# A decoder layer's convolution by parity, its norm's sums in float32r, first tokens in channel halves, MLP entry re-ordered

## The chip, the cores and the metric

The kernel runs on one core of a Trainium2 chip. The metric is the device time of one execution in microseconds (us). Three runs of the kernel before stand behind its median.

## The reference, cut to what matters

One hybrid decoder layer over 2048 tokens of 1024 channels, all in float32. Two token mixers share one input projection: an mLSTM (4 heads of 128, chunks of 128 tokens) and a causal depthwise convolution of width 31 on 512 channels with a norm over groups of 128 channels. Their outputs go through one output projection; a squared-ReLU MLP of hidden size 4096 follows.

```
h_in = rms_norm(x, pre_mix_norm_w); proj = h_in @ w_in
u = conv_val * sigmoid(conv_gate)
u = causal_depthwise_conv(u, conv_w, conv_b)          # width 31
mu = mean over 128 channels; var = mean((u - mu)^2)
y_conv = silu((u - mu) * rsqrt(var + EPS) * conv_norm_w + conv_norm_b)
x = x + rms_norm(concat(y_mlstm, y_conv) @ w_out, post_mix_norm_w)
a = relu(rms_norm(x, pre_mlp_norm_w) @ w_ff1)
x = x + rms_norm((a * a) @ w_ff2, post_mlp_norm_w)
```

## The kernel before, in words

**Arithmetic.** Every large product is made of three float32r products: each operand is rounded to a high part (ScalarE, a copy to float32r) and a low part (VectorE, the operand less its high part), and high x high, high x low and low x high are summed in PSUM. A rounding is thus a step on ScalarE and a following one on VectorE, and a transfer must have landed before.

**Phase A** (to about 590 us) makes the input projection in 96 slots, a list that is written out (SLOTS). Most slots are one PSUM bank of 128 x 512, 24 products of TensorE each. Kinds are qk, gate, val, v, o and ow. TensorE, ScalarE and VectorE each run a loop over the slots in which a function is called at a fixed slot number. ScalarE evacuates each slot but the val ones; VectorE multiplies val by the gate (glu, L811) into the ring u_buf, which has three buffers of 1024 tokens and 30 of the past. A unit is one group of 128 channels by 1024 tokens; there are eight.

**The convolution** of a unit is 31 taps: two on ScalarE (first_tap L624, second_tap L634), 29 on VectorE as operations of 1024 elements that alternate between two sums (tap L829), and one addition (L838). tap_plan (L179) hands taps out to slots: a slot gives VectorE 100 units, a tap costs 23, a weight split or a norm step 22, a q/k convolution 76. CONV_END is the slot in which a unit ends. The norm's steps stand at fixed distances from it (L162): mean sum 1, centring 2, square 3, variance sum 4, root 5, multiplication 6, silu and store to DRAM 7. For the last unit (LAST_UNIT_AT, L163) they are 0, 0, 0, 1, 1, 1, 1. The plan gives CONV_END 22, 29, 41, 49, 60, 68, 79, 87. The sums over 128 channels are float32 products with a matrix of ones (group_sum L500).

**End of phase A.** Slot 91 is CHUNK_0_SLOT. After it TensorE makes the scores of chunk 0 (L537), for which it waits for the last root and for scores_here(0) (L1195): q, k and two row loads, and for the first two chunks also chunk_here (L1191), which counts the loads of v, o and yc. SP loads yc (L1250) when both stores of the convolution's output have landed. Slots 88 to 95 are of kind ow; slot 91 writes the bank of slot 90 and waits for its evacuation.

**Start.** SP issues: x of tokens 0 to 255 (load_first, all channels), the parameters par_a, weight tiles 0 and 1, x of tokens 256 to 511, tiles 2 and 3, then the rest. ScalarE and VectorE wait for par_a, square x in pairs of channel tiles, and split the weight tiles 0 and 1. TensorE fills the wait with warm-up products of ones (WARM = 30), sums the squares, and makes 8 more (WARM_MORE).

**Phase B** (to about 850 us) handles 16 chunks of 128 tokens: mLSTM, output projection in two halves (project), norms, transposes of h2. **Phase C** is the MLP as two stages of seven products of half-sized quadrants (P1 to P7, as by Strassen). The MLP entry is where they overlap: SP loads the token quadrants of the first stage (prefetch["tokens"]), P5 in step 16 of its loop, P2, P3, P6, P7 and P4 in step 17; ScalarE rounds P2 and P3 at the end of step 16 (L1594), VectorE P2 and P3 at the start of step 17 (L1724). TensorE makes P1, the transposes of chunk 14, P2, P3, P6, P7, P4, the last transposes, P5.

**Second stage.** 56 steps, each of 48 products on one part of the hidden values (load_hid L2054, a ring of three). SP issues part 1, the last seven stores of hidden values, then at step n part n + 2 and some weight pieces called grains, which GpSimd adds.

Of the kernel before, what the change touches and what calls it, by code (L numbers as in the profile page):

```python
# [11 lines left out]
P = 128  # L12
S = 2048
# [66 lines left out]
DVE_TAPS = CW - 1  # L80
# [90 lines left out]
WARM, WARM_MORE = 30, 8  # L171
# [3 lines left out]
def convs_at(s):  # L175
    return [q for q in Q_AT if Q_AT[q] == s]


def tap_plan():  # L179
# [5 lines left out]
    for s in range(N_SLOTS):  # L185
        ready = DVE_TAPS * sum(glu_end(u) <= s for u in range(N_UNITS))
# [3 lines left out]
        ends = [min(i for i in range(s) if out[i] >= DVE_TAPS * (u + 1)) for u in range(n // DVE_TAPS)]  # L190
        for u in range(2, N_UNITS):
            if u - 2 >= len(ends) or s < ends[u - 2] + 9:
                ready = min(ready, DVE_TAPS * u)
        more = max(0, min(ready - n, room // TAP_COST))
        for u in range(U_RING, N_UNITS):
            if s + 1 >= glu_slot(u):
                more = max(more, DVE_TAPS * (u - U_RING + 1) - n)
        n += more
        room = min(room - TAP_COST * more, TAP_COST)
# [5 lines left out]

FIRST_TAP = [max(min(s for s in range(N_SLOTS) if TAPS[s] > DVE_TAPS * u) - 1, glu_end(u)) for u in range(N_UNITS)]
CONV_END = [min(s for s in range(N_SLOTS) if TAPS[s] >= DVE_TAPS * (u + 1)) for u in range(N_UNITS)]

SECOND_TAP = [max(FIRST_TAP[u], CONV_END[u - 1] if u else 0) for u in range(N_UNITS)]
# [5 lines left out]
def units_at(s, step):  # L215
    return [u for u in range(N_UNITS) if CONV_END[u] + (step if u < N_UNITS - 1 else LAST_UNIT_AT[step]) == s]
# [30 lines left out]
def phase_a(nc, sem, psum, dram, big, keep, tail):  # L247
# [3 lines left out]
    with ExitStack() as ctx:  # L251
# [9 lines left out]
        u_buf = sb("u_buf", [P, U_RING, CW - 1 + HALF])  # L261
        c_buf = sb("c_buf", [P, 2, HALF])
        th = sb("th", [P, 2, TB])
        sb("pad_a", [P, PAD_A])
# [28 lines left out]
        c_odd = sb("c_odd", [P, HALF])  # L293
        ones, eps = keep["ones"], keep["eps"]
        ln_ps = psum[:, 6:8, :].rearrange("p a b -> p (a b)")

# [38 lines left out]
        def sync(sp):  # L335
# [7 lines left out]
            def load_first(part):  # L343

                at = slice(part * PART, (part + 1) * PART)
                sp.dma_start(big["raw"][:, :, at], dram["xt"][:, :, at]).then_inc(sem["x_in"][part], 16)

            def load_x(tb):
                for half in range(2):
                    kt = slice(half * KT // 2, (half + 1) * KT // 2)  # L350
                    sp.dma_start(x_at(tb, kt), dram["xt"][:, kt, tb * TB:(tb + 1) * TB]).then_inc(sem["x_in"][2 * tb + half], 16)
# [21 lines left out]
        def tensor(pe):  # L373
# [5 lines left out]
            def sum_part(part, kt):  # L379
# [4 lines left out]
                elif kt < KT // 2:  # L384
                    pe.wait_ge(sem["x_sq"], kt // 2 + 1)
                else:
                    pe.wait_ge(sem["x_sq_dve"], (kt - KT // 2) // 2 + 1)
# [124 lines left out]
            for s in range(6, N_SLOTS):  # L512
                slot(s)
                for u in units_at(s, AT_MEAN):
                    pe.wait_ge(sem["tap"], DVE_TAPS * (u + 1))
# [4 lines left out]
                    for b in range(2):  # L520
                        group_sum(c_buf[:, u % 2], b)
# [26 lines left out]
        def scalar(act):  # L548
            def square_pair(q, part):
                act.wait_ge(sem["x_in"][part], 16)  # L550
# [73 lines left out]
            def first_tap(u):  # L624
# [1968 lines left out]
```

## Time and profile before

| | us |
|---|---|
| median of 3 runs (2085.43 to 2087.7) | 2086.36 |
| the profiled execution, its own time | 2085.33 |
| its span, first to last instruction | 2083.5 |
| TensorE busy | 2067.1 |
| VectorE busy | 1446.1 |
| ScalarE busy | 912.1 |
| GpSimd busy | 417.2 |
| mean granted TensorE clock | 0.998 |

The span lacks 1.8 us of the execution's own time, which lies around it. Products on TensorE are pipelined: a row's duration is longer than the distance to the next one, and that distance (the pitch) is what a product costs.

### The profile page before, as it was taken

The numbers are of one execution on the slowest core, as the hardware profiler recorded it, in microseconds if no ns is written. First come the engines' busy times: TensorE is split into PE (matmuls) and PEld (weight loads), VectorE is DVE, ScalarE is ACT, GpSimd is POOL, SyncE is SP. The second block draws the span as 40 slices with busy tenths as digits, with TensorE's granted clock in tenths as the row PEclk, the third lists the DMA queues.
The fourth block names the chain that finished last, engine by engine and source line by source line (L and its number), as shares of the span: only waits on it lengthen the run. The fifth ranks groups of instructions, "written<-read, shape, count | busy, mean of one in ns | idle before, by whom it ended". The sixth has DMA issues, their size and how long they took to land. (4 is left out here: it accounts for less than half of the span.)

```text
span 2083.5 us, 26901 instructions
## 1 busy us (share of the span) xinstructions
PE 2067.1 (99%) x10031; PEld 1734.2 (83%) x10031; DVE 1446.1 (69%) x1993; ACT 912.1 (44%) x1557; POOL 417.2 (20%) x252
## 2 busy tenths in 40 slices
PE   9999999999999999999999999999999999999998
PEld 8897878878788888788888888888788888888887
DVE  6897999989567777886666976666563536624285
ACT  6632434343454445754555654455331313313163
POOL 0000000000002323352332333232353134400012
PEclk9999999999999999999999999999999999999999
DMA  5121212113656875765446755545756455543376
GB/s 204 32 87 47 70 41 81 51 32 105 199 177 195 266 235 171 266 192 167 137 142 191 236 171 156 167 150 189 245 210 259 154 193 202 174 169 126 138 257 218
DMA packets 254144, 338.55 MB, mean 162 GB/s; under 512 B 11584, under 2 KB 195648, under 8 KB 240192
## 3 DMA queue, kind: packets, MB, share of 16 engines
q1 hardware_dynamic: 221376, 315.80, 45.6%
q10 hardware_dynamic: 32384, 20.98, 3.2%
q8 instruction: 81, 1.33, 0.3%
q14 instruction: 47, 0.39, 0.1%
q0 software_dynamic: 256, 0.07, 0.0%
HBM read 225.58 MB, written 111.21 MB: 162 GB/s over the span
## 5 line engine op out<-in xcount | busy, mean ns | idle before, releaser
L1978 PE MATMUL psum<-x_hi,w_hi_P 128*128 128x512 f32 x896 | 349.8, 390 | 3.8 <-DVE x_lo L1922 2.4
L2198 PE MATMUL psum<-w_hi,hid_hi 128*128 128x512 f32 x896 | 348.8, 389 | 1.9 <-DVE hid_lo L2074 1.9
L1978 PE MATMUL psum<-x_lo,w_hi_P 128*128 128x512 f32 x896 | 349.1, 390 | 0.0
L1978 PE MATMUL psum<-x_hi,w_lo_P 128*128 128x512 f32 x896 | 349.1, 390 | 0.0
L2198 PE MATMUL psum<-w_hi,hid_lo 128*128 128x512 f32 x896 | 348.6, 389 | 0.0
L2198 PE MATMUL psum<-w_lo,hid_hi 128*128 128x512 f32 x896 | 348.6, 389 | 0.0
L2074 DVE TENSOR_TENSOR hid_lo<-hid_raw,hid_hi 128x1024 fp32r<-128x1024 f32 x112 | 174.4, 1593 | 211.4 <-ACT hid_hi L2069 211.4
L1891 POOL TENSOR_TENSOR w_raw<-w_raw 128x512 f32<-128x512 f32 x128 | 184.9, 1467 | 395.3 <-DVE w_lo_P L1904 345.8
L2069 ACT ACTIVATE hid_hi<-hid_raw 128x1024 fp32r<-128x1024 f32 x112 | 112.9, 1051 | 343.4 <-DMA hid_raw<-scratch_hid 343.3
L1904 DVE TENSOR_TENSOR w_lo_P<-w_raw,w_hi_P 128x512 fp32r<-128x512 f32 x224 | 184.1, 834 | 98.1 <-ACT w_hi_P L1900 95.5
L1900 ACT ACTIVATE w_hi_P<-w_raw 128x512 fp32r<-128x512 f32 x224 | 136.0, 626 | 236.8 <-PE psum L1978 227.2
L1978 PEld LDWEIGHTS psum<-x_hi,w_hi_P 128*128 128x128 f32 x896 | 168.4, 188 | 40.4 <-issue 5.9
L2198 PEld LDWEIGHTS psum<-w_hi,hid_hi 128*128 128x128 f32 x896 | 168.2, 188 | 37.5 <-issue 2.7
L1978 PEld LDWEIGHTS psum<-x_hi,w_lo_P 128*128 128x128 f32 x896 | 168.5, 188 | 35.5
L1978 PEld LDWEIGHTS psum<-x_lo,w_hi_P 128*128 128x128 f32 x896 | 168.6, 188 | 34.7
L2198 PEld LDWEIGHTS psum<-w_hi,hid_lo 128*128 128x128 f32 x896 | 168.2, 188 | 35.0
L2198 PEld LDWEIGHTS psum<-w_lo,hid_hi 128*128 128x128 f32 x896 | 168.2, 188 | 34.9
L2030 POOL TENSOR_TENSOR w_raw<-w_raw,w_grain 128x1024 f32<-128x1024 f32 x48 | 137.9, 2888 | 224.5 <-DMA w_grain<-in_w 224.5
L841 DVE SCALAR_TENSOR_TENSOR c_buf<-u_buf,par_a,c_buf 128x1024 f32<-128x1024 f32 x120 | 153.2, 1276 | 0.0
L841 DVE SCALAR_TENSOR_TENSOR c_odd<-u_buf,par_a,c_odd 128x1024 f32<-128x1024 f32 x112 | 142.9, 1276 | 5.2 <-ACT c_odd L638 5.2
L404 PE MATMUL psum<-big_hi,w_hi 128*128 128x512 f32 (+1 forms) x288 | 109.0, 378 | 0.8 <-DVE big_lo L795 0.7
L2323 DVE TENSOR_TENSOR c<-c,psum 128x512 f32<-128x512 f32 x96 | 65.4, 681 | 61.9 <-PE psum L1978 61.9
(284 smaller groups left out, 3820.0 us busy)
## 6 DMA issues: line engine op xcount, KB each, us to landing
scratch_hid<-stage SPq DMA_DIRECT2D x224, 256.0 KB, 3.7
hid_raw<-scratch_hid SPq DMA_DIRECT2D x56, 1024.0 KB, 4.9
w_raw<-in_w SPq DMA_DIRECT2D x52, 1024.0 KB, 5.0
w_grain<-in_w SPq DMA_DIRECT2D x48, 512.0 KB, 5.3
x_raw<-scratch_h2s SPq DMA_DIRECT2D x14, 1024.0 KB, 8.4
w_raw<-in_w_in SPq DMA_DIRECT2D x22, 512.0 KB, 3.6
scratch_h2s<-h2s SPq DMA_DIRECT2D x8, 1280.0 KB, 10.1
scratch_qk<-qout ACTq DMA_DIRECT2D x16, 512.0 KB, 3.3
```

What stands on the lines that cost most here:

```text
L404: mm = nc.tensor.matmul(out, a, b, start=kt == 0 and i == 0, stop=kt == KT - 1 and i == 2)
L841: nc.vector.scalar_tensor_tensor(out=out, in0=u_buf[:, u % U_RING, k:k + HALF], scalar=par[:, CONV_W + g * CW + k:CONV_W + g * CW + k + 1] ...
L1891: nc.gpsimd.tensor_tensor(raw_1(op), raw_1(a), raw_1(b), ALU.subtract).then_inc(sem["w1_t"], 1)
L1900: nc.scalar.activation(w1_hi[op][:], raw_1(op), ACT.Copy).then_inc(sem["w1_hi"], 1)
L1904: nc.vector.tensor_tensor(w1_lo[op][:], raw_1(op), w1_hi[op][:].bitcast(F32), ALU.subtract).then_inc(sem["w1_lo"], 1)
L1978: mm = nc.tensor.matmul(psum[:, bank_1(op, g), :], l, r, start=kt == 0 and i == 0, stop=kt == 3 and i == 2)
L2030: nc.gpsimd.tensor_tensor(part, part, grain[:, n % 2], alu).then_inc(sem["w2_t"], 1)
L2069: nc.scalar.activation(hid_hi[n % HID_RING][:, half_fps(h)], hid_raw[n % HID_RING][:, half_fps(h)], ACT.Copy).then_inc(sem["hid_hi"], 1)
L2074: nc.vector.tensor_tensor(hid_lo[n % HID_RING][:, half_fps(h)], hid_raw[n % HID_RING][:, half_fps(h)], hid_hi[n % HID_RING][:, half_fps(h) ...
L2198: mm = nc.tensor.matmul(psum[:, bank, :], l, r, start=f == 0 and k == 0, stop=f == NFP - 1 and k == 2)
L2323: nc.vector.tensor_tensor(out[:], a[:], ps1(op, g), ALU.add).then_inc(sem["gather"], 1)
```

## The change

It does the following.

- The convolution works on even and odd tokens apart. u_buf holds the two halves of a unit one after the other (glu writes them with a stride). With a = even taps on even tokens, b = odd taps on odd tokens, and m = (sums of tap pairs) on (sums of token pairs), even outputs are a + b and odd outputs m - a' - b. A unit is 48 steps on VectorE with 512 or 513 elements (527 for the first) in place of 30 with 1024: S (token pairs), 15 A, 14 B, 15 M, E, T, O. Three first taps are on ScalarE. The planner charges 12.6 a step.
- The norm's sums are float32r: u is rounded to a high part (ScalarE) and a low part (VectorE), summed in two products per bank each; the same for the squares. The high part lies in the ring of u, so glu waits for the sums of three units ago, not for its taps.
- The steps stand at other distances; the planner charges four norm steps in place of one. Silu writes tokens back in order, with a stride, into another buffer.
- The first 256 tokens come as two transfers of four channel tiles each from a copy in DRAM of their own; tile 0 of the weights is loaded and split ahead of them; ScalarE squares pairs 0 and 2, VectorE 1 and 3; squares don't wait for par_a. WARM is 18.
- MLP entry: P5's tokens are loaded last; P2 is rounded earlier, on ScalarE after the squares of the first half of chunk 15, on VectorE between the two halves of post_scale. Second stage: hidden part 2 is issued before the last stores; the grains for the second product start one step later.

```
-DVE_TAPS = CW - 1
+EVEN, ODD = (CW + 1) // 2, CW // 2
+UH = HALF // 2
+UX = UH + EVEN
...
-AT_MEAN, AT_CENTER, AT_SQUARE, AT_VAR, AT_RSTD, AT_NORM, AT_SILU = 1, 2, 3, 4, 5, 6, 7
-LAST_UNIT_AT = {AT_MEAN: 0, AT_CENTER: 0, AT_SQUARE: 0, AT_VAR: 1, AT_RSTD: 1, AT_NORM: 1, AT_SILU: 1}
+UNIT_AT = {AT_HIGH: 0, AT_SUM_HIGH: 1, AT_LOW: 1, AT_SUM_LOW: 2, AT_CENTER: 2, AT_SQUARE: 3, AT_SQUARE_LOW: 3,
+           AT_VAR: 5, AT_RSTD: 6, AT_NORM: 7, AT_SILU: 8}
+LAST_UNIT_AT = {AT_HIGH: 0, AT_SUM_HIGH: 1, AT_LOW: 1, AT_SUM_LOW: 2, AT_CENTER: 2, AT_SQUARE: 2, AT_SQUARE_LOW: 2,
+                AT_VAR: 3, AT_RSTD: 3, AT_NORM: 3, AT_SILU: 3}
-TAP_COST = 23
+STEP_COST = 12.6
-WARM, WARM_MORE = 30, 8
+WARM, WARM_MORE = 18, 8
...
+    out = [("S", 0)]
+    for j in range(1, EVEN):
+        out += [("A", j)] + ([("B", j)] if j < ODD else []) + ([("M", j - 1)] if j > 1 else [])
+    return out + [("E", 0), ("M", EVEN - 1), ("T", 0), ("O", 0)]
...
-            room -= 22 * sum(out[s - AT_NORM] >= DVE_TAPS * (u + 1) > out[s - AT_NORM - 1] for u in range(N_UNITS))
+            for at in (AT_LOW, AT_CENTER, AT_SQUARE_LOW, AT_NORM):
+                room -= 22 * sum(out[s - UNIT_AT[at]] >= N_STEPS * (u + 1) > out[s - UNIT_AT[at] - 1] for u in range(N_UNITS))
...
-            if u - 2 >= len(ends) or s < ends[u - 2] + 9:
+            if u - 2 >= len(ends) or s < ends[u - 2] + 10:
...
+                for half, landed in enumerate((sem["x_in"][0], sem["x_head"])) if part == 0 else ():
+                    kt = slice(half * KT // 2, (half + 1) * KT // 2)
+                    sp.dma_start(big["raw"][:, kt, at], dram["x_first"][0, :, kt]).then_inc(landed, 16)
...
+            load_w(0)
             load_first(0)
             sp.dma_start(par[:], dram["params_a"]).then_inc(sem["par_a"], 16)
-            load_w(0)
             load_w(1)
...
-            def group_sum(src, b):
-                nc.tensor.matmul(psum[:, 6 + b, :], ones[:], src[:, b * TB:(b + 1) * TB],
-                                 start=True, stop=True).then_inc(sem["ln_sum"], 1)
+            def group_sum(src, b, start, stop):
+                return nc.tensor.matmul(psum[:, 6 + b, :], ones_r[:], src[:, b * TB:(b + 1) * TB], start=start, stop=stop)
...
                 for u in units_at(s, AT_VAR):
-                    pe.wait_ge(sem["c_sq"], u + 1)
+                    pe.wait_ge(sem["ln_act"], 3 * u + 3)
+                    pe.wait_ge(sem["ln_dve"], 3 * u + 3)
                     for b in range(2):
-                        group_sum(rstd, b)
+                        group_sum(high_part(u), b, True, False)
+                        group_sum(square_low, b, False, True).then_inc(sem["ln_sum"], 1)
...
                 if tb % 2 == 0 and u >= U_RING:
-                    dve.wait_ge(sem["tap"], DVE_TAPS * (u - U_RING + 1))
+                    dve.wait_ge(sem["ln_sum"], LN_SUMS * (u - U_RING + 1))
...
+                nc.vector.scalar_tensor_tensor(out=a_sum, in0=u_halves(u)[:, 0, j:j + UH + 1],
+                                               scalar=par[:, CONV_W + g * CW + 2 * j:CONV_W + g * CW + 2 * j + 1],
+                                               in1=a_sum, op0=ALU.mult, op1=ALU.add).then_inc(sem["tap"], 1)
...
+                    for name in ("scores", "qs", "z", "incr", "y", "yc_lo"):
+                        sp.wait_ge(sem[name], NCH - 1)
+                    prefetch["tokens"](sp, OPS[6:])
...
                     do["squares"](c - 1, 0)
+                if c == NCH:
+                    prefetch["high_x"](act, "P2")
                 if 2 <= c < NCH + 2:
                     do["pre_mlp"](c - 2)
...
                 if c == NCH + 1:
-                    prefetch["low_x"](dve, "P2")
                     prefetch["low_x"](dve, "P3")
...
                     do["post_scale"](c - 1, 0)
+                    if c == NCH:
+                        prefetch["low_x"](dve, "P2")
                     do["post_scale"](c - 1, 1)
...
         load_hid(sp, 1)
+        load_hid(sp, 2)
         store(sp, NGRP - 1)
...
-            if n + 2 < NSTEP:
+            if 1 <= n and n + 2 < NSTEP:
                 load_hid(sp, n + 2)
...
-                    if (j * 6 // n_grains if op not in WHOLE else 1 + j * 5 // n_grains) == m:
+                    if (1 + j * 5 // n_grains if op in WHOLE else 1 + j * 6 // n_grains if i == 0 else j * 6 // n_grains) == m:
```

## Rows read from the trace of the kernel before

**Rows 1.** The page, its first part: TensorE's busy time and share.

```profile
PE 2067.1 (99%) x10031; PEld 1734.2 (83%) x10031; DVE 1446.1 (69%) x1993; ACT 912.1 (44%) x1557; POOL 417.2 (20%) x252
```

**Rows 2.** Who waited for whom, TensorE: us in total, times, longest.

```profile
PE psum L1978 <- DVE x_lo L1922: 2.4, 2, 2.2
PE psum L2198 <- DVE hid_lo L2074: 1.9, 2, 0.9
PE psum L501 <- DVE c_buf L838: 1.1, 3, 0.8
```

**Rows 3.** Timeline of TensorE, 156 to 163 us: start, us, what.

```profile
157.74 1.88 PE L501 MATMUL psum<-c_buf,ones 128*128 128x512 f32 x4
...
159.68 0.39 PE L404 MATMUL psum<-big_lo,w_hi 128*128 128x512 f32 x1
159.91 0.39 PE L404 MATMUL psum<-big_hi,w_lo 128*128 128x512 f32 x1
```

**Rows 4.** Timeline of VectorE, two taps of unit 0 after each other.

```profile
113.33 1.28 DVE L841 SCALAR_TENSOR_TENSOR c_buf<-u_buf,par_a,c_buf 128x1024 f32<-128x1024 f32 x1
114.53 1.28 DVE L841 SCALAR_TENSOR_TENSOR c_odd<-u_buf,par_a,c_odd 128x1024 f32<-128x1024 f32 x1
```

**Rows 5.** VectorE by line (busy us, mean ns, idle before); then busy time from 95 to 540 us.

```profile
L800 DVE SCALAR_TENSOR_TENSOR x_raw<-x_raw,par_a,rstd_a 128x512 f32<-128x512 f32 x16 | 11.7, 744 | 8.2 <-ACT rstd_a L571 8.2
...
95.00:540.00 445.00, 443.86 (x2400) 377.47 (x2399) 398.01 (x368) 166.80 (x193) 4.15 (x10) 1.00 0.22 69
```

**Rows 6.** Timeline of TensorE, end of slot 87 and slot 91 to the scores.

```profile
537.95 0.39 PE L480 MATMUL psum<-w_hi,big_lo 128*128 128x512 f32 x1
...
559.97 0.47 PE L480 MATMUL psum<-w_hi,h_hi 128*128 128x512 f32 x1 [0.78 <-ACT th L615]
...
565.54 1.06 PE L1389 MATMUL psum<-q_t,k_t 128*128 128x128 f32 x8
```

**Rows 7.** Timelines of ScalarE, SP and VectorE: slot 88's evacuation to the exponents.

```profile
546.58 0.60 ACT L615 ACTIVATE th<-psum 128x512 f32<-128x512 f32 x1 [3.15 <-PE psum L480]
...
552.39 1.25 ACT L713 ACTIVATE c_buf<-c_buf,par_a 128x1024 f32<-128x1024 f32 x1
...
557.91 0.80 SPq L1250 DMA_DIRECT2D yc_c<-scratch_yc  x2
...
560.79 2.25 DVE L1207 SCALAR_TENSOR_TENSOR p_c<-negm_b,cols,mask 128x128 f32<-128x128 f32 x4 [8.46 <-DMA yc_c<-scratch_yc]
```

**Rows 8.** MLP entry: TensorE, VectorE; busy time by engine, PEclk, DMA, GB/s.

```profile
853.92 0.47 PE L1978 MATMUL psum<-x_hi,w_hi_P 128*128 128x512 f32 x1 [2.21 <-DVE x_lo L1922]
...
874.30 0.47 PE L1978 MATMUL psum<-x_hi,w_hi_P 128*128 128x512 f32 x1 [0.66 <-DVE h2s L1699]
...
851.16 0.32 DVE L1670 TENSOR_TENSOR small<-small 128x1 f32<-128x1 f32 x1 [1.75 <-ACT junk L1529]
...
852.11 6.16 DVE L1922 TENSOR_TENSOR x_lo<-x_raw,x_hi 128x1024 fp32r<-128x1024 f32 x4
...
854.00:858.40 4.40, 4.39 (x12) 3.04 (x13) 4.40 (x4) 3.31 (x5) 0.92 (x1) 0.61 1.05 387
```

**Rows 9.** Timelines at the start: TensorE, ScalarE, VectorE.

```profile
9.87 1.99 PE L388 MATMUL psum<-c_buf,ones 128*128 128x256 f32 x8
...
9.19 1.16 ACT L551 ACTIVATE c_buf<-big_raw 128x512 f32<-128x512 f32 x2 [7.16 <-DMA par_a<-in_params_a]
...
10.49 1.06 ACT L581 ACTIVATE w_hi<-w_raw 128x1024 fp32r<-128x1024 f32 x1 [0.15 <-DMA w_raw<-in_w_in]
...
11.82 1.06 ACT L581 ACTIVATE w_hi<-w_raw 128x1024 fp32r<-128x1024 f32 x1 [0.27 <-DMA w_raw<-in_w_in]
...
14.59 0.88 DVE L800 SCALAR_TENSOR_TENSOR big_raw<-big_raw,par_a,rstd_a 128x256 f32<-128x256 f32 x2 [0.45 <-ACT rstd_a L571]
```

**Rows 10.** Second stage: TensorE's third step; SP's issue of hidden part 2.

```profile
1488.51 0.47 PE L2198 MATMUL psum<-w_hi,hid_hi 128*128 128x512 f32 x1 [0.93 <-DVE hid_lo L2074]
...
1479.87 0.72 SPq L2062 DMA_DIRECT2D hid_raw<-scratch_hid  x1
```

More of the change, by code:

```diff
@@ L513, in tensor @@
                 slot(s)
-                for u in units_at(s, AT_MEAN):
-                    pe.wait_ge(sem["tap"], DVE_TAPS * (u + 1))
+                for u in units_at(s, AT_SUM_HIGH):
+                    pe.wait_ge(sem["ln_act"], 3 * u + 1)
                     if u == 0:
@@ L549, in square_pair @@
             def square_pair(q, part):
-                act.wait_ge(sem["x_in"][part], 16)
+                if part == 0 and q >= KT // 4:
+                    act.wait_ge(sem["x_head"], 16)
+                else:
+                    act.wait_ge(sem["x_in"][part], 16)
                 nc.scalar.activation(x_sq_pair(q, part), x_pair(q, part), ACT.Square).then_inc(sem["x_sq"], 1)
@@ L718, in scalar @@
                     act.dma_start(dram["yc"][chunks(half), :, g, :].rearrange("c p t -> p c t"),
-                                  c_buf[:, u % 2].rearrange("p (c t) -> p c t", t=P)).then_inc(sem["c_out"][u % 2], 16)
+                                  c_tokens(u)[:].rearrange("p (c t) -> p c t", t=P)).then_inc(sem["c_out"][u % 2], 16)
+                for u in range(N_UNITS):
+                    if FIRST_TAP[u] == s:
+                        first_taps(u)
+                    if PAIR_TAP[u] == s:
+                        pair_tap(u)
                 for j, half in convs_at(s - 2):
@@ new lines, in odd_tap @@
+            def odd_tap(u, j):
+                g = u // 2
+                if j == 1:
+                    dve.wait_ge(sem["tap0"], 3 * u + 2)
+                else:
+                    dve.wait_ge(sem["tap"], step_done(u, "B", j - 1))
+                nc.vector.scalar_tensor_tensor(out=b_sum, in0=u_halves(u)[:, 1, j:j + UH],
+                                               scalar=par[:, CONV_W + g * CW + 2 * j + 1:CONV_W + g * CW + 2 * j + 2],
+                                               in1=b_sum, op0=ALU.mult, op1=ALU.add).then_inc(sem["tap"], 1)
@@ new lines, in pair_tap, with add_pairs @@
+            def pair_tap(u, j):
+                if j == 1:
+                    dve.wait_ge(sem["tap0"], 3 * u + 3)
+                else:
+                    dve.wait_ge(sem["tap"], step_done(u, "M", j - 1))
+                nc.vector.scalar_tensor_tensor(out=m_sum(u), in0=u_pairs(u)[:, j:j + UH], scalar=pair_weight(u // 2, j),
+                                               in1=m_sum(u), op0=ALU.mult, op1=ALU.add).then_inc(sem["tap"], 1)
+            def add_pairs(u):
+                dve.wait_ge(sem["evac"]["dve"], 2 * (u + 1))
+                if u >= 1:
+                    dve.wait_ge(sem["tap"], step_done(u - 1, "M", EVEN - 1))
+                nc.vector.tensor_tensor(u_pairs(u), u_halves(u)[:, 0, 1:UX], u_halves(u)[:, 1, 0:UX - 1],
+                                        ALU.add).then_inc(sem["tap"], 1)
@@ new lines, in even_tokens, with both_sums, odd_tokens @@
+            def even_tokens(u):
+                dve.wait_ge(sem["tap"], step_done(u, "A", EVEN - 1))
+                nc.vector.tensor_tensor(c_buf[:, u % 2, 0:UH], a_sum[:, 0:UH], b_sum, ALU.add).then_inc(sem["tap"], 1)
+            def both_sums(u):
+                dve.wait_ge(sem["tap"], step_done(u, "E"))
+                nc.vector.tensor_tensor(b_sum, a_sum[:, 1:UH + 1], b_sum, ALU.add).then_inc(sem["tap"], 1)
+            def odd_tokens(u):
+                dve.wait_ge(sem["tap"], step_done(u, "T"))
+                nc.vector.tensor_tensor(m_sum(u), m_sum(u), b_sum, ALU.subtract).then_inc(sem["tap"], 1)
@@ new lines, in add_weights @@
+            def add_weights():
+                taps = par[:, CONV_W:CONV_W + H * CW].rearrange("p (g k) -> p g k", g=H)
+                sums = pairs[:, 0:H * EVEN].rearrange("p (g j) -> p g j", g=H)
+                nc.vector.tensor_tensor(sums[:, :, 0:ODD], taps[:, :, 0:CW - 1:2], taps[:, :, 1:CW - 1:2], ALU.add)
+                nc.vector.tensor_copy(sums[:, :, ODD:EVEN], taps[:, :, CW - 1:CW])
+                link(nc.vector.tensor_scalar(pairs[:, H * EVEN:H * EVEN + H], par[:, CONV_B:CONV_B + H], 2.0, None, ALU.mult))
@@ L863, in vector @@
                 nc.vector.memset(qk_raw(j, 0)[:, 0:QW - 1], 0.0).then_inc(sem["q_head"], 1)
-            for q in range(KT // 4, KT // 2):
-                square_pair(q)
-            split_w(0)
             split_w(1)
@@ L1324, in sync @@
                     load_x(c)
-                if c == NCH:
-                    for name in ("scores", "qs", "z", "incr", "y", "yc_lo"):
-                        sp.wait_ge(sem[name], NCH - 1)
-                    prefetch["tokens"](sp, OPS[6:])
                 if c == NCH // 2:
```

215 lines of the change are left out of this document (141 added, 74 removed).

## The prediction

> **What bounds the kernel now.** I read the page's first part first: TensorE is busy for 99% of the span [rows 1]. So a change pays only where it removes TensorE work or one of its few waits. The waits of TensorE [rows 2] name three places that the change touches: the MLP entry (2.4 us), the start of the second MLP stage (1.9 us) and the sums of the convolution's norm (1.1 us). VectorE has slack: 398.0 us busy of 445 us between 95 and 540 us [rows 5]. A cheaper convolution on VectorE is therefore worth nothing by itself.
>
> **Norm sums, seven units.** A float32 sum is two recorded passes. Four records, that is two sums, start at 157.74; the second L404 product starts at 159.68 and one pitch before that is 159.45, so two sums hold TensorE for 1.71 us, 0.855 us each [rows 3]. The float32r products follow each other at 0.23 us (159.68 to 159.91). A unit now has 4 sums, two for the mean and two for the variance, 3.42 us. It gets 8 float32r products, 8 x 0.23 = 1.84 us. Gain 1.6 us a unit, 11.2 us for units 0 to 6. Of the 1.1 us of waits for c_buf [rows 2], 0.3 us belong to them and go, since the sums now stand one slot later.
>
> **The last unit.** Here the change adds a wait. Walking the planner's loop with 48 steps at 12.6 and the four norm charges, the convolution of unit 7 still ends in slot 87. Before, its variance sum stood after slot 88 and its silu in slot 88. After, high, low, two mean steps and the low square are in between: variance, root and silu stand in slot 90. Chunk 0's scores stay after slot 91, and scores_here makes TensorE wait for chunk_here(0), which counts the load of yc, which starts when the silu has been stored. The chain from the evacuation of slot 88 to the landing is 546.58 to 560.79, 14.2 us, with silu at 552.39 and the load's issue at 557.91 [rows 7]. TensorE had 19 us for it and came 4.7 us late (565.54 [rows 6]). Now it hangs on slot 90, and TensorE needs from there 0.9 us for four sums (these cover the 0.78 us for which it now waits for the evacuation) and 5.6 us for slot 91 (559.97 to 565.54 [rows 6]), 6.5 us: **it waits about 7.7 us**. As a whole: before, end of slot 87 (537.95 + 0.23) to the scores is 27.4 us. After: 3 slots x 5.5 + 4 early products 0.9 + 14.2 = 31.6 us. Loss 4.2 us, this unit's cheaper sums and the vanished 0.8 us wait included. Queued behind on SP are the second half of w_out (needed two slots later, covered) and on POOL and VectorE scale_q and the exponents, which then run beside slot 92.
>
> An idle TensorE also loses its clock: after the gap that ended at 853.92 the granted clock of 854 to 858.4 was 0.61 in the mean, so the lower level (1.2 GHz) lay over some 0.78 x 4.4 = 3.4 us, 1.7 us lost [rows 8]. I add 1.7 us behind the longer gap: +5.9 us in all. The Trainium skill (TensorE: Matmul & The Clock Gate, "What's actually happening") says the same from the other side: throttled is the default and only activity releases it. Without that rule and row the sum would be 1.7 us lower.
>
> **VectorE and the ring of u.** A unit's taps go from 30 operations of 1.28 us, which follow each other at 1.20 us [rows 4], about 36 us, to 48 of half the length. The nearest row is a 512-element one with a column scalar, 744 ns [rows 5]; less the same 0.08 us of overlap 0.66 us, about 31.5 us a unit. The two added 1024-long subtractions (no more than 1.2 us each, the pitch of a tap of that length) leave 2 us of gain a unit, all in slack. ScalarE gets two roundings of 1.06 us [rows 9] a unit and saves half a us, also slack. But glu of slot 45 must now wait for the sums of unit 2, which stand after slot 46, because the high part lies in the ring of u. Behind it queue 20 steps of unit 3 (13 us), the glu of slot 47, a weight split and a norm. Counted through, unit 3 ends some 6 us into slot 50, and TensorE waits for its rounding after slot 50: between 0 and 3 us, I take 1.0.
>
> **Start.** The sums of the first 256 tokens begin at 9.87, when par_a (9.19) has landed, and w tile 0 is there at 10.49, tile 1 at 11.82 [rows 9]. After, tile 0 goes ahead of x, squares wait for x halves only and not for par_a, and both roundings of tile 0 lie ahead of them; but ScalarE's root stands behind the rounding of tile 1. If transfers keep their pace, tile 1 lands at 11.8 as now, the root follows at 12.9 and VectorE can normalise at 14.1 instead of 14.59: 0.5 us. If the smaller first transfer lets the queue start quicker, up to 3.3 us. Against it: 18 warm-up products instead of 30 end near 6.4 us; with the sums at 9.4 the clock would have fallen, which costs up to 1.5 us in place of a gain. I take a gain of 1.5, ends -1.5 and +3.3. The split into halves in DRAM costs nothing: rows in SBUF stay 1 KB.
>
> **MLP entry.** TensorE waits 2.21 us until 853.92 for the low part of P2, then runs partly at the low clock, then waits 0.66 us before 874.30 for VectorE's h2s [rows 8]. P5's load (1 MB; at the 387 GB/s of this stretch [rows 8] 2.7 us) goes behind P4's, so P2 lands 2.7 us earlier than now; its rounding fits into ScalarE's idle time before pre_mlp(14), or delays it by up to 1 us. From 852.11 to 874 us VectorE is busy almost without a break, and the same work remains. What it can give back is its 1.75 us of idle time before 851.16 [rows 8], no more; PE's 2.2 us and the clock are then paid by later small waits. Gain 1.75, ends 0 and 3.9 (all of gap and clock). P5's own roundings come 15 us later and don't notice.
>
> **Second stage.** Hidden part 2 is issued at 1479.87 behind seven stores and lands so late that TensorE starts at 1488.51 after 0.93 us [rows 10]; part 3 the same. Issued ahead of the stores and of the grains, both are early: -1.9 us. The grains move back one step and still end before step 7, when their roundings start.
>
> **Sum.** -11.2 -0.3 +5.9 +1.0 -1.5 -1.75 -1.9 = -9.75 us. The profiled execution took 2085.33 us (span 2083.5, 1.8 us around it), so 2075.6; the median of the runs is 1.0 us above it: **2076.5 us**.
>
> **Rivals.** (1) *No wait at the scores*: if the yc chain is hidden (a load that I count wrongly, a planner end some slots earlier), the seam gives 1.6 + 0.8 + 0.8 us instead of costing 5.9: 2067.5 us. For it: 4.7 us of slack now. Against it: two slots of 5.5 us eat more than that. Chance 0.18. (2) *Small gain*: start loses 1.5, the entry gives nothing, unit 3's wait is 3: -9.75 + 3.0 + 1.75 + 2.0 = -3.0, 2083 us. Chance 0.09. (3) *VectorE becomes the bound, slower*: the half-length taps cost more than the planner's 12.6% of a 5.47 us slot (0.69 us), and every unit's high part is late for its sum. The nearest row gives 0.66 us, so only 4% lie between. 384 steps at 0.80 are 54 us more than mine; against 47 us idle time now, 16 us gained and more synchronising waits, some 20 us would reach TensorE: about 2095 us. It decides from about 0.75 us a step. The Trainium skill (VectorE: DVE Perf Modes, "The TRN2 errata") speaks against short operations, since each pays a fixed latency anew. The rows have that term as 2 x 0.744 - 1.28 = 0.21 us, and 0.66 us includes it; hence only 0.05.
>
> **Numbers.** Forecast case 0.68. The range takes in rivals 1 and 2: 2065 to 2083. About 0.2%, 4.2 us, is what a measurement of this kernel tells from no change. Faster: forecast and rival 1, 0.86 less a tail, 0.85; within: 0.10; slower: 0.05.
>
> **What would show it.** Norm sums in float32r at some 0.23 us pitch, 64 of them; a TensorE gap of 6 to 9 us before L1389's first score ended by yc or what waits for it, and the lower clock level behind it; no gap at 1488 or 1500; the P2 product right behind its transposes, small waits for x_lo of P3 to P7 instead; steps at 0.66 us. Wrong would be: no gap at the scores (then 2067), or waits for the high part in every unit (then slower).

## The result: slower by 0.6%, and the profile after

The changed kernel takes 2098.14 us (median of 4 runs, 2097.42 to 2100.17), the kernel before beside it 2086.56: ratio 1.0058, 95% interval [1.0046, 1.007]. The forecast was 2076.5 us, so the change is slower by 11.6 us where it was to be faster by 10. The profiled execution of after has a span of 2097.0 us against 2083.5.

The page of after, its first part, against [rows 1]: TensorE has 6 us less to do and VectorE 14 us less, and still the span is 13.5 us longer.

```profile
PE 2060.8 (98%) x10007; PEld 1740.2 (83%) x10007; DVE 1432.2 (68%) x2164; ACT 929.0 (44%) x1581; POOL 419.0 (20%) x252
```

The waits of TensorE in after (us in total, times, longest), against [rows 2]: the 1.1 us before the norm's sums have become 18.4 us in three lines, there is a new wait at the scores, and the wait for the hidden part is gone.

```profile
PE psum L558 <- DVE u_high L1038: 8.5, 3, 5.9
PE psum L558 <- ACT u_high L770: 5.5, 3, 3.6
PE psum L1544 <- DMA yc_c<-scratch_yc: 5.3, 1, 5.3
PE psum L558 <- DVE square_low L1046: 4.4, 1, 4.4
PE psum L2135 <- DVE x_lo L2079: 1.8, 1, 1.8
```

The timeline of TensorE gives the large ones their places: unit 4's high sum, unit 6's low sum, unit 7's variance sums, the scores.

```profile
380.42 1.22 PE L558 MATMUL psum<-u_high,ones 128*128 128x512 f32 x2 [3.59 <-ACT u_high L770]
...
506.76 1.22 PE L558 MATMUL psum<-u_high,ones 128*128 128x512 f32 x2 [5.90 <-DVE u_high L1038]
507.78 0.41 PE L546 MATMUL psum<-w_hi,big_hi 128*128 128x256 f32 x1
507.99 0.41 PE L546 MATMUL psum<-w_lo,big_hi 128*128 128x256 f32 x1
...
512.58 0.28 PE L546 MATMUL psum<-w_hi,big_hi 128*128 128x256 f32 x1
512.70 0.28 PE L546 MATMUL psum<-w_lo,big_hi 128*128 128x256 f32 x1
...
566.48 0.50 PE L558 MATMUL psum<-high_last,ones 128*128 128x512 f32 x1 [4.40 <-DVE square_low L1046]
...
579.96 1.40 PE L1544 MATMUL psum<-q_t,k_t 128*128 128x128 f32 x5 [5.28 <-DMA yc_c<-scratch_yc]
```

The four products in the middle show the clock. Behind the 5.9 us gap products of 256 columns follow each other at 0.21 us, from about 512.2 us on at 0.12 us. These are the two levels, 1.2 and 2.4 GHz. The granted clock was 0.5 for 6.8 us from 379.1, 6.8 from 505.3, 3.4 from 566.8 and 6.8 from 577.0. Windows of after say the same (the last three columns are PEclk, DMA share, GB/s):

```profile
505.00:513.00 8.00, 6.24 (x30) 6.05 (x31) 8.00 (x11) 1.15 (x1) 0.14 (x2) 0.57 0.31 98
566.00:570.00 4.00, 3.52 (x9) 2.84 (x10) 0.33 (x1) 2.90 (x3) 0.00 (x0) 0.60 0.18 66
577.00:584.00 7.00, 4.04 (x16) 3.81 (x17) 2.91 (x5) 1.74 (x6) 1.26 (x1) 0.51 0.76 237
```

**Where the 13.5 us of span are**, from start times of the same products in both traces. To the first product: 16.12 to 14.20, -1.9 us. From there to the scores (565.54 and 579.96): +16.3. Scores to the first product of MLP stage 1 (847.57 and 863.87): +1.9, in it the low clock behind the scores' gap. Stage 1: -0.4. Stage 2: -2.5. So all of the loss is made between the first product and the scores. There the waits for sums grew by 17.3 and the scores' by 5.3 us, cheaper sums gave 8 x 1.6 = 12.8 back, one wait of 0.8 went, and 7.3 us are left. The low clock explains 6.4 of them, 0.9 us stay unexplained: of its first 17.1 us TensorE worked through 14.3, and a product took 0.213 instead of 0.118 us, so 0.45 of that time is lost. Of the last 6.8 us, 3.9 lie behind the scores and explain 1.7 of the 1.9 us there.

The rows that answer to [rows 4], [rows 8] and [rows 9]: two kinds of half-length steps on VectorE (by line), then TensorE's first product, and its first P2 product at the MLP entry.

```profile
L920 DVE SCALAR_TENSOR_TENSOR ab_buf<-u_buf,par_a,ab_buf 128x513 f32<-128x513 f32 x120 | 90.0, 750 | 4.0 <-ACT ab_buf L695 4.0
L931 DVE SCALAR_TENSOR_TENSOR ab_buf<-u_buf,par_a,ab_buf 128x512 f32<-128x512 f32 x112 | 83.8, 748 | 0.0
```

```profile
14.20 0.36 PE L461 MATMUL psum<-big_hi,w_hi 128*128 128x256 f32 x1 [0.84 <-DVE big_lo L877]
...
873.36 0.47 PE L2135 MATMUL psum<-x_hi,w_hi_P 128*128 128x512 f32 x1 [1.80 <-DVE x_lo L2079]
```

The steps have the duration that was forecast, the first product comes 1.9 us earlier, and the wait at the entry is still 1.8 us. The wait that was in [rows 10] has no row in after.

### The profile page after: what moved, and what is told of

Read it like the earlier page. It is cut to its first block, busy times and chain, and to the rows that moved or that the text cites. A ratio compares the mean times of both kernels' runs of the same rounds, so it can differ in the third digit from the quotient of the medians.

```text
span 2097.0 us, 27079 instructions
## 1 busy us (share of the span) xinstructions
PE 2060.8 (98%) x10007; PEld 1740.2 (83%) x10007; DVE 1432.2 (68%) x2164; ACT 929.0 (44%) x1581; POOL 419.0 (20%) x252
## 4 chain that ended last, share of the span: by engine, by line
PE 57%; DVE 1%; issue 0%; ACT 0%; DVEq 0%; ACTq 0%
PE psum L2356 29%; PE psum L2135 28%; DVE x_lo L2079 0%; DVE w_lo_P L2061 0%; DVE c L2481 0%; DVE c_x L2481 0%; ACT x_hi L2072 0%; ACT junk L1693 0%; DVE xn L1838 0%; DVE h2s L1855 0%; DVE acc L2562 0%; DVE acc L2540 0%; DVEq L2703 0%; ACT rs_c L2411 0%; ACT junk_c L2438 0%
## 5 line engine op out<-in xcount | busy, mean ns | idle before, releaser
L461 PE MATMUL psum<-big_lo,w_hi 128*128 128x512 f32 (+1 forms) x288 | 105.3, 366 | 0.0
L461 PE MATMUL psum<-big_hi,w_lo 128*128 128x512 f32 (+1 forms) x288 | 105.3, 366 | 0.0
```

Source lines behind the costliest of these rows:

```text
L461: mm = nc.tensor.matmul(out, a, b, start=kt == 0 and i == 0, stop=kt == KT - 1 and i == 2)
```

## Experiments

The table has for each run the time from the first product (L404 of before) to the first score in its profiled execution, the stretch in which all of the loss is made, beside the median. The other stretches, the start aside, differ by 2.5 us at most. With the new start the first product comes between 13.0 and 14.3 us, which differs from execution to execution. The kernel before, run beside each group, had medians from 2085.7 to 2086.6 us (2086.2 is that of all its runs), so medians of different groups compare to about 1 us.

| run | what it is | first product to scores, us | median, us |
|---|---|---|---|
| before | | 549.4 | 2086.2 |
| after | | 565.8 | 2098.1 |
| e1 | start, entry, stage 2 only | 550.4 | 2082.3 |
| e2 | after, float32 sums | 550.9 | 2082.0 |
| e3 | after, float32 sums in unit 7 | 560.2 | 2088.7 |
| e4 | after, own root buffer in unit 7 | 564.8 | 2096.3 |
| e5 | e3 + filled gaps | 556.3 | 2088.7 |
| e6 | e3 + low part earlier in its slot | 552.4 | 2083.3 |
| e7 | e3 + joint mean sum | 555.9 | 2087.0 |
| e8 | e3 + q/k ahead of first taps | 560.6 | 2090.6 |
| e9 | e6 + VectorE's load cut | 537.1 | 2067.9 |
| e10 | e6 + q/k stored from the raw rows | 542.4 | 2073.6 |
| e11 | e7 + the same | 544.8 | 2074.9 |
| e12 | after + the same | 556.1 | 2089.3 |
| e13 | e1 + the same | 548.4 | 2079.0 |

The theory at the start: the sums in float32r are what loses, since each unit's mean now goes ScalarE, TensorE, VectorE, TensorE (each step a handshake with the next) with one slot between, on queues served in order. Rivals: the parity convolution puts VectorE late; the seam, the stretch from unit 7's end to the scores, is late by its DMA; the re-ordered loads cost something.

**e1, all of the change but convolution and norm.** The kernel before with only the edits of start, MLP entry and second stage:

```diff
+ sp.dma_start(big["raw"][:, kt, at], dram["x_first"][0, :, kt]).then_inc(landed, 16)
...
+ if c == NCH:
+     prefetch["high_x"](act, "P2")
...
+ load_hid(sp, 2)
```

> The kernel before with the change's start, MLP entry and second-stage edits only; convolution and norm as before. Theory (the loss is made by the convolution's and norm's part alone): the start gives 1.9 us (first product at 14.2 instead of 16.1), the second stage 1.9, the entry 0 to 1.5, so 2081 to 2083 us, and a clock below full only behind the entry. Rival (some of the loss is made by the moved loads): 2086 us or more.

Measured 2082.29 us, ratio 0.998 [0.9971, 0.9989]. As expected: these parts are worth 4 us, and none of the loss is theirs.

**e2, the parity convolution with float32 sums.**

```diff
- group_sum(high_part(u), b, True, False).then_inc(sem["ln_sum"], 1)
+ exact_sum(c_buf[:, u % 2], b).then_inc(sem["ln_sum"], 2)
...
+ root_last = ab_buf[:, 0:HALF]
```

> The changed kernel with the parity convolution, but the norm's sums taken in float32 straight from the float32 tiles in all 8 units, at the slots of the kernel before (no high and low parts, variance 4 slots after the convolution's end, last unit 0 and 1 slots after it); the last unit's squares and root stand in the buffer of the two partial sums, so that they don't wait for the store of unit 6. Theory (handshakes of the split sums make the waits, the half-length steps are harmless): all of the 18 us of waits for sums and the 5 us at the scores go, and with them the low clock of phase A; what stays is the gain of start and second stage: 2081 to 2084 us. Rival (the parity convolution itself puts VectorE late): waits of several us for the sums of units 3 to 7 remain, 2088 us or more.

Measured 2081.98 us, 0.998 [0.9971, 0.9989], the same as e1. The parity convolution neither helps nor hurts by itself with float32 sums, and the float32r sums with their slots and buffers, cheaper by 12.8 us, cost 16 us net.

**e3, float32 sums for the last unit alone.** The same edit with `exact(u)` true for unit 7 only.

> The changed kernel with float32 sums, at the slots of the kernel before, for the last unit only (its squares and root in their own buffer as in the run above); units 0 to 6 keep the split sums. Theory: the 4.4 us before the variance sums and the 5.3 us before the scores go, with some 3 to 5 us of low clock, against 1.6 us more for the sums: 2086 to 2090 us; the waits of units 2 to 6 (14 us) and their low clock stay. Rival (the seam is late because unit 7's convolution is late, whatever its sums are): 2094 us or more, with a wait of over 4 us at the sums or scores.

Measured 2088.71 us, 1.0012 [1.0003, 1.0021]: of the 16 us the seam makes 9.4. By the profiles it is 7.8: 5.6 up to the scores and 2.2 between the scores and MLP stage 1. From unit 7's first sum to the scores it takes 26.4 us again (546.83 to 573.26), as before (539.09 to 565.54), against 29.95 in after, where the first sum also stands a slot later. e3 is the base for the runs that follow.

**e4, without the wait for unit 6's store.**

```diff
- nc.scalar.activation(rstd[:], c_buf[:, u % 2], ACT.Square).then_inc(sem["ln_act"], 1)
+ nc.scalar.activation(root(u), c_buf[:, u % 2], ACT.Square).then_inc(sem["ln_act"], 1)
...
+ sp.wait_ge(sem["c_out"][0], 16 * (N_UNITS // 2))
```

> The changed kernel with one wait removed: squares, low squares and root of the last unit stand in the buffer of the two partial sums instead of the one from which unit 6 is stored, so ScalarE's squares no longer wait 6.2 us for that store to land; the k load of the tail waits for the store instead. Theory (that store is what makes the variance sums 4.4 us late): variance sums on time, the scores' wait falls to 0 to 5 us, some of the low clock goes: 2088 to 2093 us. Rival (the handshakes are late by themselves, or the yc load is): within 2 us of the changed kernel.

A miss: 2096.29 us, 1.0049 [1.0037, 1.0062], only 1.9 us better. The timeline of after shows the wait that it takes away, and the waits of e4 show why little came of it: the variance sums were on time, but the scores then waited longer for yc.

```profile
562.93 1.06 ACT L776 ACTIVATE rstd_a<-c_buf 128x1024 f32<-128x1024 f32 x1 [6.17 <-DMA scratch_yc<-rstd_a]
565.11 1.23 DVE L1046 TENSOR_TENSOR square_low<-rstd_a,high_last 128x1024 fp32r<-128x1024 f32 x1 [7.25 <-ACT high_last L779]
```

```profile
PE psum L1554 <- DMA yc_c<-scratch_yc: 7.3, 1, 7.3
```

From unit 7's first sum to the scores e4 needs 27.4 us and after 29.95, so the store's wait is worth 2.5 us there. (The table shows 1.0, since this execution of e4 had 3.4 us more of low clock, at unit 3.) The rest of the seam's loss stays without the store's wait, and e3, with the sums and slots of the kernel before, has none of it. That fits the seam's length in slots, as the prediction had it.

**e5, the low clock taken away, the waits left.** In three gaps of e3 products of the tile of ones fill TensorE's time:

```diff
+ if u == 4:
+     fill(s, 14)
...
+ if u in (3, 6):
+     fill(s, 7 if u == 3 else 24)
```

> Base: the run with float32 sums for the last unit only (2088.7 us). In the three largest gaps that TensorE has there before a norm sum (unit 3's low sum 1.9 us, unit 4's high sum 3.7 us, unit 6's low sum 5.9 us) 7, 14 and 24 products of the tile of ones with itself are put ahead of the wait; they write a free bank and change no result. The waits end when they ended before. Theory (the idle gaps also cost the clock behind them: 17 us at 0.5 in that run): the low stretches go and 6 to 9 us with them, 2080 to 2083 us. Rival (the low clock costs next to nothing, what counts is the waits alone): 2087 us or more.

Measured 2088.70 us, 1.0014 [1.0005, 1.0023]: nothing, by the medians. Yet the edit did what it was meant to: the windows below, of e3 first and then of e5, have a granted clock of 0.89 and 0.81 against 1.00 and 0.95.

```profile
370.00:400.00 30.00, 26.19 (x179) 24.75 (x178) 26.50 (x42) 8.21 (x11) 0.00 (x0) 0.89 0.18 50
497.00:515.00 18.00, 12.12 (x79) 11.72 (x78) 12.43 (x14) 5.58 (x7) 0.14 (x2) 0.81 0.28 87
```

```profile
370.00:400.00 30.00, 28.60 (x212) 26.72 (x211) 27.34 (x46) 7.48 (x10) 0.00 (x0) 1.00 0.21 70
497.00:515.00 18.00, 18.00 (x147) 17.91 (x147) 13.36 (x16) 5.24 (x7) 0.14 (x2) 0.95 0.28 88
```

In e3 the clock was low for 17 us of the stretch up to the scores, and TensorE worked through 14.8 of them; in e5 it was low for 3.4. At the pitches above some 5 us of TensorE's time came back. By the profiles, from the first product to the scores e5 is 3.9 us shorter. Part of the rest is the edit's own: the fill ahead of unit 6's low sum runs 0.7 us past the end of the low part. And part is waited away. From unit 4's high sum to unit 6's, e3 has a low stretch that costs 2.6 us and e5 has none, yet both need 114.1 to 114.2 us. In e5 TensorE meets these waits, where e3 has none and one of 1.0 us:

```profile
387.88 0.73 PE L576 MATMUL psum<-u_high,ones 128*128 128x512 f32 x2 [1.28 <-DVE u_high L1083]
...
494.31 0.73 PE L576 MATMUL psum<-u_high,ones 128*128 128x512 f32 x2 [2.12 <-ACT u_high L812]
```

Why the 3.9 us don't show in the medians stays open. In the profiled execution of e5 the first product comes 1.2 us later than in e3's and MLP stage 1 takes 1.8 us more, both outside the edit, and its runs scatter (2086.7 to 2092.5). My theory in its first form, waits plus clock, has no place for a gain that is waited away. **The second theory:** between unit 2 and unit 7 VectorE's queue sets the pace, by its work plus forced waits; what TensorE gains there is waited away at a later sum. The waits of VectorE from 95 to 545 us, in the kernel before and in after, show what there is:

```profile
DVE u_buf L825 <- PE psum L404: 25.8, 11, 7.6
DVE qout L852 <- ACT qout L649: 13.2, 8, 4.3
```

```profile
DVE qout L1000 <- ACT qout L719: 29.4, 8, 7.8
DVE u_buf L910 <- PE psum L461: 8.5, 4, 4.2
DVE u_buf L910 <- issue: 7.9, 3, 5.0
DVE u_buf L903 <- PE psum L558: 7.5, 1, 7.5
DVE square_low L1046 <- ACT u_high L779: 6.2, 3, 3.4
```

VectorE is busy 21 us less than before in this stretch (399.2 and 378.2 us), but before it mostly waited for TensorE to finish a glu slot (25.8 us), which costs nothing. Now it waits for qout, for the ring of u, for the squares. And the timelines of ScalarE and VectorE show the wait for qout from inside, at unit 6:

```profile
493.26 1.06 ACT L770 ACTIVATE u_high<-c_buf 128x1024 fp32r<-128x1024 f32 x1 [5.03 <-DVE c_buf L965]
...
496.25 1.14 ACT L725 ACTIVATE qout<-qout,par_a 128x1024 f32<-128x1024 f32 x1
497.42 0.37 ACTq L728 DMA_DIRECT2D scratch_qk<-qout  x1
500.46 1.15 ACT L719 ACTIVATE qout<-qraw,par_a 128x1024 f32<-128x1024 f32 x1 [3.07 <-DMA scratch_qk<-qout]
```

```profile
501.64 3.92 DVE L1000 SCALAR_TENSOR_TENSOR qout<-qraw,par_a,qout 128x1024 f32<-128x1024 f32 x3 [7.80 <-ACT qout L719]
505.49 1.22 DVE L1038 TENSOR_TENSOR u_high<-c_buf,u_high 128x1024 fp32r<-128x1024 f32 x1
```

ScalarE waits 5.0 us for the convolution's last step, because the rounding of the high part stands first in its slot. Queued behind it are three first taps and the silu of the q/k convolution before. Its store goes out at 497.4, and the next first tap, into the same qout, waits for it to land. VectorE waits 7.8 us for that tap, and only then comes the low part for which TensorE has waited since 500.9. The next runs test links of this chain.

**e6, the low part ahead of the q/k convolution.**

```diff
+ for u in split_at(s, AT_LOW):
+     dve.wait_ge(sem["ln_sum"], LN_SUMS * u + 2)
  for j, half in convs_at(s - 1):
      convolve_qk(j, half)
```

> Base: as above, 2088.7 us. One thing moved: on VectorE the low part of units 0 to 6 stands ahead of the q/k convolution of its slot, not behind it. Theory (unit 6's 5.9 us and unit 3's 1.9 us are a low part queued behind a q/k convolution, which itself waits for ScalarE's first tap and so for the store of qout): both waits go, and the low clock of 506 us and 318 us: 2078 to 2082 us; unit 4's 3.7 us for the high part stay. Rival (VectorE is simply behind, the order doesn't matter): 2087 us or more, the waits stay.

Measured 2083.31 us, 0.9986 [0.9978, 0.9995], 5.4 us less than e3 and 1.3 us above the expected range. The waits at units 3 and 6 went, but TensorE was earlier and met another one, at unit 7's mean sum:

```profile
PE psum L576 <- ACT u_high L800: 5.4, 3, 3.5
PE psum L579 <- issue: 5.1, 1, 5.1
```

**e7, two handshakes fewer.** The low part goes into the buffer of the roots and all four mean sums stand together:

```diff
- nc.vector.tensor_tensor(high_part(u), c_buf[:, u % 2], high_part(u).bitcast(F32),
+ dve.wait_ge(sem["c_out"][(u - 1) % 2], 16 * ((u - 1) // 2 + 1))
+ nc.vector.tensor_tensor(square_low[:], c_buf[:, u % 2], high_part(u).bitcast(F32),
```

> Base: as above, 2088.7 us. The split mean sum with two handshakes fewer: the low part goes into the buffer of the roots instead of over the high part, so that it need not wait for the sums of the high part; it stands ahead of the q/k convolution; all four sums of the mean stand together 2 slots after the convolution's end, so the high part has two slots and the low part one. Nothing else of units 0 to 6 moves. Theory: all waits of units 2 to 6 (14 us) and their low clock (8 us) go, 2066 to 2073 us, below both kernels. Rival (a wait in another form takes their place, for the store of the unit before which the roots' buffer must see landed, or the ring): 2078 us or more.

A miss: 2087.04 us, 1.0003 [0.9994, 1.0012], 17 us above the middle of what I expected. TensorE's waits for sums are no shorter than in e6, in other places (7.9 us in three, 5.2 at unit 7), and VectorE waits 7.8 us for the store of the unit before. More room in slots for the handshake did not help here. The edit also added the wait for the store, so e7 alone does not show which of the two undid the gain.

**e8, the first taps behind q/k on ScalarE**, in the order of the kernel before:

```diff
  for j, half in convs_at(s):
      first_tap_qk(j, half)
+ for u in range(N_UNITS):
+     if FIRST_TAP[u] == s:
+         first_taps(u)
```

> Base: as above, 2088.7 us. One thing moved: on ScalarE the first taps of a unit stand behind the q/k silu, store and first tap of the slot, as in the kernel before, not ahead of them. Theory (VectorE idles 29 us for qout's first tap instead of 13 us because the store that this tap waits for is issued later): VectorE's idle time for qout falls by 10 us or more, unit 4's high part is earlier by some of it, 2083 to 2087 us. Rival (these waits are the store's own time, or the steps wait for the first taps instead): within 1.5 us of 2088.7.

Measured 2090.55 us, 1.0018 [1.0009, 1.0026]: no gain. The 1.8 us above e3 lie within the scatter of its runs (2086.2 to 2091.7). VectorE's idle time for qout fell only from 31.2 to 27.8 us.

**e9, VectorE with less to do.**

```diff
+ b = b_sum[:, 0:64] if j >= 8 else b_sum
...
+ m = m_sum(u)[:, 0:64] if j >= 8 else m_sum(u)
```

> Base: the run with the low part ahead of the q/k convolution (2083.3 us). Left out: of the odd taps and of the pair taps with number 8 and up, in all units, only the first 64 of 512 columns are computed; number, order and waits of the instructions stay. VectorE has some 15 x 0.6 = 8 us less to do in a unit, TensorE and ScalarE the same as in the base. Theory (between units 2 and 7 it is VectorE's in-order work with its forced waits that sets when the high part and unit 7's mean sum can come; what TensorE saved in the sums turned up there as waits, 3.5 us at unit 4 and 5.1 us at unit 7): these waits go, with their low clock, 2069 to 2074 us. Rival (the waits come from the slots in which the steps stand, not from VectorE's load): 2081 us or more.

The kernel leaves out seven eighths of the columns of 15 taps in each unit; VectorE is busy for 325 us between 95 and 545 us, against 380 in e6. Measured 2067.94 us, 0.9915 [0.9901, 0.9929], 15.4 us below e6 and a little below what was expected. From the first product to the scores it takes 13.3 us less than e1: seven units' cheaper sums (11.2 us) and e1's waits for c_buf (2.2 us). What TensorE still waits for at the sums of units 0 to 6 in the whole trace is one row:

```profile
PE psum L576 <- DVE u_high L1071: 0.5, 1, 0.5
```

Nothing was changed but VectorE's load: the handshakes, the slots and ScalarE's queue are those of e6. So in e6 VectorE, its work plus its forced waits, is the bound of this stretch, and 2068 us is about what these sums are worth when it isn't. Its waits by themselves cost nothing once it has time for them: the one for qout is longer here than in e6 (22.7 us), and the one for the ring of u is 7.5 us in both.

```profile
DVE qout L1035 <- ACT qout L749: 34.2, 10, 6.8
```

**e10, the q/k store no longer blocks qout.**

```diff
- nc.scalar.activation(qout[:], qout[:], ACT.Silu,
+ nc.scalar.activation(qk_raw(j, half)[:, QW - 1:QW - 1 + HALF], qout[:], ACT.Silu,
...
- act.wait_ge(sem["q_out"], 16 * (2 * j + half))
+ act.wait_ge(sem["q_silu"], 2 * j + half)
```

> Base: as above, 2083.3 us. The silu of a q/k convolution writes into the raw rows that it came from, and is stored from there; ScalarE's next first tap into qout no longer waits for the store before it, only the next fill of the raw rows does. VectorE idled 23 us in the base for that tap, 13 us in the kernel before. Theory (as above, and this wait is a part of it that can be removed): VectorE's idle time for qout falls to under 15 us, the waits at unit 4's high part and unit 7's mean sum (3.5 and 5.1 us) shrink by half or more, 2074 to 2080 us. Rival (VectorE idles there because TensorE has not finished the slot, the store is only what is seen last): 2082 us or more.

Measured 2073.55 us, 0.9941 [0.9929, 0.9954]: 9.8 us below e6, just below the expected range. **This version beats both kernels**, the one before by 12 us and the changed one by 25; its last unit has float32 sums. Its waits, VectorE's and then TensorE's:

```profile
DVE qout L1038 <- ACT qout L750: 9.1, 5, 4.8
```

```profile
PE psum L576 <- DVE u_high L1074: 1.7, 2, 1.3
PE psum L576 <- ACT u_high L803: 1.7, 2, 0.9
PE psum L579 <- issue: 1.4, 1, 1.4
```

VectorE's work is the same as in e6; its wait for qout fell from 22.7 to 9.1 us. The clock has no low stretch before the end.

**e11, the same on e7.**

> Base: the run with the joint mean sum (2087.0 us), with the same change of the q/k store. Theory: as above, some 4 to 8 us less, 2079 to 2083 us; it stays above the run with the separate sums and the same store, since VectorE's low part still waits for the store of the unit before (7.8 us in the base), which holds up all that is queued behind it. Rival: 2086 us or more.

Measured 2074.88 us, 0.9951 [0.9937, 0.9965]: 12.2 us gained where 4 to 8 were expected. The order of the two (e10 ahead) is as expected, but by 1.3 us only, so the wait for the unit's store (7.8 us on VectorE here too) mattered less than I thought.

**e12, the q/k store alone, on the changed kernel.**

> The changed kernel (2098.1 us) with the change of the q/k store alone: silu of q and k into their raw rows, stored from there. Theory (VectorE's chain sets the sums of units 3 to 7, and the wait for the store is its largest removable part): some 8 to 12 us less, 2086 to 2090 us, unit 4's and unit 6's waits smaller; the last unit's seam (variance sums waiting for unit 6's store, yc at the scores) stays, 5 us or more of gaps. Rival (that wait matters only once the low part stands ahead of the q/k convolution): 2094 us or more.

Measured 2089.26 us, 1.0013 [1.0004, 1.0022]: 8.9 us of the 11.6 that after loses. The two waits of 3.6 and 5.9 us shrank (the longest at a sum of units 0 to 6 is 2.2 us); the seam stays, as expected:

```profile
PE psum L558 <- DVE square_low L1051: 4.6, 1, 4.6
PE psum L1549 <- DMA yc_c<-scratch_yc: 4.1, 1, 4.1
```

**e13, the q/k store on e1**, with float32 sums and the old taps.

> The kernel before with the start, entry and second-stage edits (2082.3 us) and the change of the q/k store; float32 sums and the old taps. Theory (with float32 sums TensorE is slow enough for VectorE; only the waits for c_buf, 2.2 us, can go): 2080 to 2082 us. Rival (the store's wait costs TensorE time in every version of this kernel): 2077 us or less.

Measured 2078.97 us, 0.9965 [0.9952, 0.9977]: 3.3 us less than e1, between the two expectations. Waits for c_buf fell from 2.2 to 0.4 us. So even with the long sums VectorE's chain cost TensorE something.

## Why the prediction was wrong, step by step

By the medians the 21.6 us between forecast and result (2076.5 and 2098.1) divide like this: 16.9 are units 0 to 6 (+6.4 from e1 to e3, where -11.2 - 0.3 + 1.0 = -10.5 was forecast), 3.5 the seam (+9.4 from e3 to after instead of +5.9), 1.2 start, entry and second stage (e1).

- **"VectorE has slack": the step that failed.** The prediction read 398 us busy of 445 as slack, took it over to the changed kernel, and put all waits of units 0 to 6 there at 1.0 us. They are 14.0 us, with two low stretches of the clock of 6.8 us each behind them. e9 shows that there was no slack: less load on VectorE and nothing else is worth 15 us. The sentence behind it in the prediction, that a cheaper convolution is worth nothing by itself, holds with float32 sums (e2 against e1) and not with split ones. The sign was in rows I had: the c_buf waits of the kernel before [rows 2], 1.1 us in three places, are the convolution's end coming just at the sum (unit 7's last addition ends at 539.0 us, its sum starts at 539.09). A wait of 0.8 us says that two engines run level there, and e1 bears it out: with an earlier start and nothing else changed ahead of it, this wait grew to 1.8 us. Make TensorE 1.6 us a unit quicker, and it waits for VectorE.
- **Norm sums, -11.2 us.** The price was right: pitch, 8 products a unit, 12.8 us of TensorE time with unit 7. The credit was not. On e1 and e2 as they are it came to a loss; with the q/k store out of the way about half of it is there (e13 to e10: 5.4 us, with the parity convolution and the split sums' own waits in it), and all of it with VectorE lightened (e13 to e9: 11.3 us from the first product to the scores).
- **Unit 3's wait, 1.0 us.** It measured 0.9 for the high and 1.9 for the low part. The units that I did not walk through, 2, 4 and 6, had another 11 us. I followed what queues behind the glu of slot 45, and not what queues behind ScalarE's new first instruction in a slot, the high rounding: the q/k silu and its store.
- **The last unit, +5.9 us.** Mechanism and place right (silu and root two slots later, yc ends the wait), size short. From the end of slot 87 to the scores 33.3 us with the clock were predicted; the first sum of unit 7 at 550.0 less one slot of 5.5 gives 35.5. The waits were 4.4 + 5.3 instead of 7.7 us: the prediction had no line for ScalarE's wait for unit 6's store. Without it, in e4, the same stretch is 27.4 + 5.5 = 32.9 us and the wait for yc 7.3, both close to the forecast. The clock was low for 10 us instead of 3.4. e3: 9.4 us for the whole seam.
- **The clock, +1.7 us.** 8 us in the ledger. Such a term is not simply additive: ahead of a wait that another engine ends, a faster clock buys in part a longer wait. In e5 3.9 of some 5 us came through to the scores, with 0.7 lost to the fill. MLP stage 1 shows it without any fill: it takes 617.67 us in after, with 3.4 us of low clock at its entry, and 617.67 us in e1 with none, where TensorE instead waits 0.5 and 0.6 us more for low parts. The Trainium skill (TensorE: Matmul & The Clock Gate, "What's actually happening") says that activity releases the throttle. e5's windows agree: with the gaps filled the granted clock is 1.00 and 0.95 instead of 0.89 and 0.81.
- **Start -1.5:** -1.9, right, though 1.5 was picked between ends of -1.5 and +3.3, other executions with the same start give 1.8 to 3.1, and in e1 1.0 us is waited away before the scores (549.4 to 550.4 us). **Second stage -1.9:** -2.5, right, and the wait for hid_lo is gone. **MLP entry -1.75:** -0.4; the P2 wait is 1.8 us instead of 2.2, the one for h ahead of it grew from 0.2 to 0.9 us, and the clock was low for 3.4 us again. e1 as a whole is worth 4.0 us where these steps said 5.2.
- **VectorE's steps:** 0.66 us pitch (750 ns each), and 14 us less work in all: right. Of the rivals the third, slower at 2095 us with VectorE as the bound and every high part late, came nearest, though from another cause: not dearer steps but their neighbours' waits. It got 0.05, because I had tied it to the price of a step alone, and that its 2095 us lie near the measured time is luck.

What stays open: how the seam could be kept short with split sums (every run that mended it went back to float32 there), and what part of VectorE's load is the added rounding and what part its forced waits, beyond the one for the q/k store.

## What to carry to other kernels

An engine's idle time is slack only if none of it is a wait in a chain that ends at the bounding engine; look whether its results arrive just in time, and if so, treat both as the bound. Where a new instruction that waits is put first in an in-order queue, list what stands behind it, above all a DMA whose landing someone needs. And when a step's cost is to be credited to the end time, lighten the second engine in an experiment first: it tells at once what the step could be worth.

## What was not expected of the hardware

With the clock kept through 14 of 17 us of low stretches the median did not move (e5, 2088.70 and 2088.71 us), and a low stretch of 3.4 us in MLP stage 1 left the stage as long as without it (617.67 us in after and e1). A wait of 1.9 us at the MLP entry had no low clock behind it in e1, while 1.8 us had in after (3.4 us from 874.0); the length of one gap alone does not tell it.
